# One attention break per step: transposes, next scores and older values behind a unit

## The reference

```python
def diff_attention(q1, q2, k1, k2, v, lam):          # 4 heads, 64 wide; v 128 wide
    ...
        def probs(q, k):
            s = jnp.einsum('bhqd,bhkd->bhqk', q, k).astype(jnp.float32) * scale
            return jax.nn.softmax(jnp.where(mask, s, NEG_INF), axis=-1)

        att = probs(qb1, k1) - lam * probs(qb2, k2)   # one block of 128 queries
        return jnp.einsum('bhqk,bhkd->bhqd', att.astype(v.dtype), v)

# in each of the two layers
    proj = u @ w_in[i]
    ...
    o = diff_attention(q1, q2, k1, k2, v, lam)
    o = rms_norm_2(o, sub_norm_g[i]) * (1.0 - lam_init)
    ...
    merged = (g_a * (y_a @ w_pool_out[i])
              + g_b * (y_b @ w_conv_out[i])
              + g_c * (y_c @ w_attn_out[i]))
    h = h + merged @ w_o[i]
```

## Time and profile before

| | |
|---|---|
| median of 3 runs | 2577.78 us (2577.49 to 2578.59) |
| the profiled execution's own time | 2577.84 us |
| its span in the trace | 2576.1 us |
| PE busy | 2558.5 us, 99% of the span |
| DVE, POOL, ACT busy | 1486.3, 1514.9, 838.6 us |
| `L_MIX` and `L_MERGE` up to the last turn_out | about 966 to 1240 us (layer 0), 1804 to 2075 us (layer 1) |

### The profile page before, as it was taken

One profiled execution on the slowest core, in us unless ns is written; L12 is line 12 of the kernel. 1 busy time (PEld: TensorE's weight loads), 2 busy tenths in 40 slices (PEclk: granted clock), 3 DMA queues, 4 the chain that ended last, 5 costly groups with the idle time before them and its releaser, 6 DMA issues.

```text
span 2576.1 us, 32876 instructions
## 1 busy us (share of the span) xinstructions
PE 2558.5 (99%) x11723; PEld 2062.5 (80%) x11723; DVE 1486.3 (58%) x2084; ACT 838.6 (33%) x1157; POOL 1514.9 (59%) x1820
## 2 busy tenths in 40 slices
PE   8999999999999999999999999999999999999999
PEld 7767778888888887778888888888778888888887
DVE  7756774487474737845583442754773448344275
ACT  5444442233222343354321111134334432111112
POOL 7634446666666755555565655765554556565576
PEclk9999999999999999999999999999999999999999
DMA  5311113222222332222322222233222222222223
GB/s 208 115 66 50 55 61 131 98 83 98 99 97 98 109 111 82 83 82 82 106 99 98 98 97 92 89 114 105 77 85 84 82 106 98 99 98 97 92 89 130
DMA packets 36829, 247.44 MB, mean 96 GB/s; under 512 B 4464, under 2 KB 4848, under 8 KB 7792
## 3 DMA queue, kind: packets, MB, share of 16 engines
q1 hardware_dynamic: 34704, 238.57, 26.2%
q10 hardware_dynamic: 2016, 7.35, 0.8%
HBM read 243.81 MB, written 2.10 MB: 95 GB/s over the span
## 4 chain that ended last, share of the span: by engine, by line
PE 31%; POOL 30%; issue 22%; DVE 0%; POOLq 0%; DMA 0%; ACT 0%; DVEq 0%; SPq 0%; ACTq 0%
POOL w_lo L377 30%; PE bank L832 7%; PE bank L834 7%; PE bank L833 7%; PE both L833 3%; PE both L834 3%; PE both L832 3%; PE bank L1281 0%; PE both L1257 0%; PE bank L1243 0%; PE bank L1241 0%; PE bank L1242 0%; DMA raw<-stream 0%; POOLq L415 0%; POOLq L374 0%
## 5 line engine op out<-in xcount | busy, mean ns | idle before, releaser
L377 POOL TENSOR_TENSOR w_lo<-raw,w_hi 128x256 fp32r<-128x256 f32 x1784 | 1492.6, 868 | 964.2 <-ACT w_hi L434 963.2
L434 ACT ACTIVATE w_hi<-raw 128x1024 fp32r<-128x1024 f32 x446 | 469.1, 1056 | 981.6 <-PE bank L834 476.8
L832 PE MATMUL bank<-a_hi,w_hi 128*128 128x512 f32 x1440 | 582.1, 404 | 0.0
L834 PE MATMUL bank<-a_hi,w_lo 128*128 128x512 f32 x1440 | 562.3, 390 | 0.0
L833 PE MATMUL bank<-a_lo,w_hi 128*128 128x512 f32 x1440 | 561.3, 390 | 0.0
L832 PEld LDWEIGHTS bank<-a_hi,w_hi 128*128 128x128 f32 x1440 | 270.5, 188 | 63.7 <-issue 10.3
L834 PEld LDWEIGHTS bank<-a_hi,w_lo 128*128 128x128 f32 x1440 | 270.3, 188 | 58.3
L833 PEld LDWEIGHTS bank<-a_lo,w_hi 128*128 128x128 f32 x1440 | 270.9, 188 | 54.7 <-issue 3.1
L832 PE MATMUL bank<-y_hi,w_hi 128*128 128x512 f32 x696 | 272.4, 391 | 0.0
L834 PE MATMUL bank<-y_hi,w_lo 128*128 128x512 f32 x696 | 270.9, 389 | 0.0
L833 PE MATMUL bank<-y_lo,w_hi 128*128 128x512 f32 x696 | 270.8, 389 | 0.0
(11 more groups left out here) (343 smaller groups left out, 3279.6 us busy)
## 6 DMA issues: line engine op xcount, KB each, us to landing
raw<-stream SPq DMA_DIRECT2D x223, 1024.0 KB, 4.8
h<-xT SPq DMA_DIRECT2D x8, 256.0 KB, 5.9
h<-xT ACTq DMA_DIRECT2D x1, 2048.0 KB, 8.1
outT<-h SPq DMA_DIRECT2D x8, 256.0 KB, 2.3
h<-decay ACTq DMA_DIRECT2D x1, 1024.0 KB, 4.8
h<-rope ACTq DMA_DIRECT2D x1, 1024.0 KB, 9.3
prob<-pT ACTq DMA_DIRECT2D x2, 512.0 KB, 4.4
par<-par ACTq DMA_DIRECT2D x2, 408.0 KB, 3.3
```

The source lines that it names most:

```text
L377: pool.tensor_tensor(w_lo[:, s, part], raw[:, s, part], w_hi[:, s, part], ALU.subtract).then_inc(lo_done, 1)
L434: act.activation(w_hi[:, s, cols], raw[:, s, cols], ACT.Copy).then_inc(hi_done, 1)
L832: pe.matmul(dst, w_hi[:, s, cols], rhs_hi(k), start=start and k == 0, stop=False)
L834: ins = pe.matmul(dst, w_lo[:, s, cols], rhs_hi(k), start=False, stop=stop and k == nk - 1)
```

## The change

Three things move, in both layers; no instruction is added or removed.

- The transposes of step s leave the inside of the unit. Behind the unit stand now, by the new function `attention_place`, the transposes of s, the scores of s+1 and the values of s-1. Only for step 15 does the place lie inside a unit (n = 23), and values(15) follow behind that unit.
- As the values of a head's last step come one step later, the head's parts move: `attention_out` and `head_root` by two slots (head 0) or three units (heads 1 and 2), `head_norm` from iterations k = 9, n = 2, n = 14 to k = 11, n = 6, n = 18, `turn_out` from slot 10, n = 3, n = 15 to slot 12, n = 7, n = 19, `head_out` with it. Head 3 stays.
- `turn_out` and the late norm's sum, which write `b_cmp`, now also wait until ACT has copied the transposes in front.

```diff
@@ -761,7 +761,7 @@
                     if k == 0:
                         load_table(ACT.Exp)
                         attention_step(0)
-                    if k == 8:
+                    if k == 10:
                         head_root()
                         load_table(ACT.Exp)
                     if k % 2 == 1:
@@ -772,7 +772,7 @@
                     if n < 24 and n % 3 == 0:
                         attention_step(8 + n // 3)
                     ahead(ub, j)
-                    if n in (1, 13, 25):
+                    if n in (4, 16, 25):
                         head_root()
                     if (layer, n) == (0, 9):
                         load_table(ACT.Sqrt)
@@ -1260,7 +1260,7 @@

                 def attention_transposes(s):

-                    if s > 1 and s % QT == 1:
+                    if s > 2 and s % QT == 2:
                         pe.wait_ge(head_out_split, layer * LAYER_HEADS + s // QT)
                     if (layer, s) == (0, 11):
                         pe.wait_ge(late_root_ready, 1)
@@ -1272,8 +1272,6 @@
                 def attention_values(s):

                     hd, i = s // QT, s % QT
-                    if s < 15:
-                        attention_scores(s + 1)
                     pe.wait_ge(probs_copied, ptr.due())
                     if i == 0:
                         pe.wait_ge(attention_out_read, ofree.due())
@@ -1283,8 +1281,17 @@
                                         skip_group_check=True)
                     ins.then_inc(values_added, pv.up())

+                def attention_place(s):
+
+                    attention_transposes(s)
+                    if s < 15:
+                        attention_scores(s + 1)
+                    if s > 0:
+                        attention_values(s - 1)
+
                 def turn_out(hd):

+                    pe.wait_ge(probs_copied, ptr.now() + (hd < 3))
                     pe.wait_ge(head_scaled, layer * LAYER_HEADS + hd + 1)
                     for i in range(QT):
                         ins = pe.transpose(b_cmp[:, i * P:(i + 1) * P], tile_c[:, i * P:(i + 1) * P], ident)
@@ -1298,10 +1305,8 @@
                 def mixed(slot, k):


-                    if k == 1 and slot == 10:
+                    if k == 1 and slot == 12:
                         turn_out(0)
-                    if k == 5 and slot % 2 == 1:
-                        attention_transposes(slot // 2)
                     if k == 3 and slot in (3, 4, 6, 8):
                         pe.wait_ge(to_transpose, tin.due())
                         g = 3 if slot == 3 else 4 - slot // 2
@@ -1313,17 +1318,18 @@
                     unit(ul + L_MIX, slot, 2, [bank[slot % 2][:, :]], a_op(), 8,
                          lambda k, slot=slot: mixed(slot, k))
                     if slot % 2 == 1:
-                        attention_values(slot // 2)
+                        attention_place(slot // 2)

                 def merged_beside(n, k):


-                    if (n, k) in ((3, 2), (15, 2), (26, 5)):
+                    if (n, k) in ((7, 2), (19, 2), (26, 5)):
                         turn_out(1 + n // 12)
                     if (layer, n) == (0, 9) and k == 1:
+                        pe.wait_ge(probs_copied, ptr.now() + 1)
                         square_sum(b_cmp, src=tile_d)
-                    if n < 24 and n % 3 == 2 and k == (3 if n % 6 > 3 else 5):
-                        attention_transposes(8 + n // 3)
+                    if (n, k) == (23, 3):
+                        attention_place(15)

                 for n in range(36):
                     br, j = n // 12, n % 6
@@ -1338,8 +1344,10 @@
                     else:
                         unit(ub, n % 12, 7 - j, [merge_bank[2 * j - 8][:, :], merge_bank[2 * j - 7][:, :]],
                              y_op(br * 4), 4, beside_n)
-                    if n < 24 and n % 3 == 2:
-                        attention_values(8 + n // 3)
+                    if n < 23 and n % 3 == 2:
+                        attention_place(8 + n // 3)
+                    if n == 23:
+                        attention_values(15)
                 singles(ul + L_WO, 8, y_op(), first=next_y, lags=first_lags, ways=2, late=2)
                 uc = ul + L_MLP
                 singles(uc, 8, a_op(), first=next_a, normed=True)
@@ -2192,15 +2200,15 @@
                         mix_in(k - 1)
                     if k % 2 == 0:
                         step_probs(k // 2)
-                    if k == 8:
+                    if k == 10:
                         attention_out()
                     if k > 0:
                         mix(k - 1)
                     if k in (3, 4, 6, 8):
                         pooled_out(3 if k == 3 else 4 - k // 2)
-                    if k == 9:
+                    if k == 11:
                         head_norm(0)
-                    if k == 10:
+                    if k == 12:
                         head_out(0)
                 mix_in(15)
                 mix(15)
@@ -2248,12 +2256,12 @@
                             head_out(3)
                         if stepped:
                             step_probs(8 + n // 3)
-                        if n in (0, 12, 24):
+                        if n in (3, 15, 24):
                             attention_out()
                         hd = 1 + n // 12
-                        if n < 24 and n % 12 == 2:
+                        if n < 24 and n % 12 == 6:
                             head_norm(hd)
-                        if n < 24 and n % 12 == 3:
+                        if n < 24 and n % 12 == 7:
                             head_out(hd)
                         if layer == 0:
                             late_norm(n)
```

## The result

The changed kernel takes 2594.14 us (median of four runs, 2590.37 to 2595.79); the kernel before took 2577.88 beside it (2577.49 to 2578.59). The ratio is 1.0061 with an interval of 1.0043 to 1.0078: slower by 0.6%, and above the range of 2584.4 to 2593.0, though two of the four runs lie inside it. The four runs lie 5.4 us apart, those of before 1.1. TensorE's granted clock, averaged over a run, was 1.000 in the run of 2590.37, 0.998 in that of 2592.65, and 0.997 in those of 2595.62 and 2595.79.

What follows compares the result with a forecast made beforehand. PE, busy for 2558.5 of 2576.1 us, bounds the kernel. Waits of turn_out (+13.0) and saved breaks (-1.2) give +11.8 us on 2577.84, so 2589.6 us, with a range of 2584.4 to 2593.0.

Steps and rivals of the forecast that it cites:

- lost whole: On PE: whatever makes it stop is lost at its length, since no later wait would take it up.
- third rival: PE resumes at a lower rate behind turn_out's waits, losing 1.6 us per stop: 2592.8 or 2596.0 us; chance 0.10.
- the cheaper form of the lower rate: Only the two 3.1 us waits of head 2 make PE resume slowly: 2589.6 + 3.2 = 2592.8 us.
- The waits of `turn_out`: PE waits for head_norm in each layer: 1.2 (head 0), 2.2 (head 1), 3.1 us (head 2); +13.0 in all.
- Head 0: Slot 12: PE waits 1.2 us for the scaled tile, DVE taking 11.6 us behind step_probs of step 5; lower bound 0.
- The longer wait: Head 2, n = 18: three long DVE instructions could each wait 0.76 us for POOL; 4.3 us, total time 2592.
- first rival: At n = 6 the head is scaled in time, only the breaks remain: 2576.6 us; chance 0.06.
- the forecast's own range: 2587.5 to 2592 us: head 0 between 0.4 and 1.4, head_norm's products short or long; chance 0.65.
- The late norm's sum: Layer 0, n = 9: head_out of head 1 precedes its squares on DVE; taken at 0, at worst 0.69 us once.
- The breaks: Steps 0 to 14 of each layer lose one break of a unit by transposes: 30 times 0.04, -1.2 us.
- Transposes to scores: Scores following directly on transposes on PE: taken at nothing, bounded at 3.3 us; as rival 2592.9 us, chance 0.03.
- The other edits at nothing: ACT's later copy, the w_hi behind it and DVE's lateness in slots 12 to 15: no cost to PE.

Runs made afterwards that it cites:

- e4: Changed kernel with unread identity transposes ahead of PE's wait for the scaled head (7, 19, 28 for heads 0, 1, 2): 2590.1 us, ratio 1.0048.
- e8: e2 with the late norm's squares of tile 4 moved to iteration 2 and of tile 5 to iteration 3 on DVE: 2577.62 us (one run).
- e1: Changed kernel with the transposes of heads 0 to 2 and the late norm's sum later inside the same units on PE: 2577.31 us, ratio 0.9998.
- e5: Changed kernel with transposes of heads 0 to 2 between units (behind slot 12, units 7, 19) and the late norm's sum at k=4: 2576.41 us, ratio 0.9995.
- e2: Changed kernel with DVE's head_norm of heads 1 and 2 ahead of the evacuation of units 6 and 18: 2579.42 us, ratio 1.0007.
- e3: Kernel before, with unread DVE products ahead of the scaling (four for head 1, five for head 2): 2595.41 us, ratio 1.0067.
- e6: Changed kernel with DVE's head_norm of heads 1 and 2 between the evacuation of units 6 and 18 and step_probs: 2582.7 us, ratio 1.0018.
- e7: Kernel before, with unread DVE products ahead of scaling heads 1 and 2: 3 and 6 in layer 0, 8 and 12 in layer 1: 2602.52 us (one run).

## Why the prediction was wrong

**The step that failed** is the price of a stop: "lost whole", so at its length, with nothing in the sum for the slow restart behind it, which took 6.0 us in the profiled run. The prediction had that restart only as its third rival, "the stops cost more than their length", at a chance of 0.10, with the range's upper end at "the cheaper form of the lower rate". Its mechanism decided in three of the four runs. Its price was nearly right: the prediction read 1.6 us per stop from the program's start, which gave 2592.8 to 2596.0; the trace has 1.6, 1.6 and 2.7 (transposes included), and the runs end at 2595.8. What was wrong was to give the likeliest case a stop that costs its length, on no better ground than that the trace had no stop of two or three us in mid program. That absence was no evidence for the cheap case, while the one place in the trace where PE came out of standing still spoke for the dear one. (The distances alone show it there; the profile's granted clock reads 1.00 in that stretch.) The section "Why this matters for your kernels" of the Trainium skill's page "TensorE: Matmul & The Clock Gate" warns of idle stretches. The trace agrees behind three of the four longer stops, with 0.43 us between two products behind one of 2.1 us. e4 shows that work in the gap keeps the clock at 1.0.

**The waits of `turn_out`**: the mechanism was right, six times in PE's list and four of over 2 us. Head 1 measured 2.11 for 2.2, head 2 3.15 for 3.1. For head 1 this was partly luck: the product took 0.69 us, not the 0.90 that was taken, and the 0.15 us from the product's end to PE's start (1116.94 to 1117.09), which the sum left out, made up for most of it. Head 0 was too large, 0.73 for 1.2, a term mis-sized by DVE durations beside POOL: from the end of `step_probs` to the scaled tile it took 10.8 us, not 11.6, since the split took 2.4 for 3.14 and the product 0.69 for 0.90. POOL, which before worked from 1037.06 to 1044.45, now stood still from 1038.94 to 1041.23 and was done at 1045.12. Sum 12.0 for 13.0. The longer wait that the prediction worked out, as a bound, from the section "Who interferes with whom" of the Trainium skill's page "SBUF — State Buffer" (4.3 us for head 2) is not in the trace; the rows' price held. Two slips change nothing: the "four instructions" of the first rival are six, and the forecast's own range ends at 2592, where the conditions that it names reach 2577.84 + 2 x 6.7 - 1.2 = 2590.0.

**The late norm's sum**, taken at 0 and bounded at 0.69 us, cost 1.58. `head_out` is two instructions of 0.75, not one, and it pushed four more, of 1.1 to 1.25 us beside POOL, past the end of unit 8, so that an evacuation and the last squares came late behind them. The bound counted the instruction that was moved, and not the queue behind it at its new place. e8 (one run) confirms it.

**The breaks**, -1.2: e1 without its two waits is 1.4 us below before, and e5 1.3, of which three more breaks in each layer (0.24 by the prediction's price) are not the change's. So -1.1 to -1.4, as forecast, as far as medians can tell: the intervals of both ratios still hold 1. **Transposes to scores**, taken at 0: no loss remains for it in e1 or e5; right. **The other edits at nothing** (the copy on ACT, w_hi, late evacuations in slots 12 to 15): none appears in the list of waits.

Without the clock the terms add up to 2577.8 - 1.2 + 12.0 + 1.6 = 2590.2, which is e4 (2590.1) and the one run at a clock of 1.000 (2590.37), 0.6 above the forecast. That this sum came out so near is luck: heads 1.0 us too dear and a late norm's sum 1.6 us too cheap nearly cancel.

## What to carry to other kernels

Where one engine is busy for 99%, an instruction moved on a second engine is costed by all that stands ahead of it in its new queue and by all that is queued behind it; the loss here was repaired by asking 2 to 5 us later on PE (e1, e5), or, for the longer stops, by DVE's order alone (e2). A stop of PE of over some two us in mid program is costed at its length plus a slow restart, which came behind 9 of 11 such stops in the three traces that have them and took 1.3 to 2.7 us. And a kernel whose runs spread where they did not before is one in which to read the granted clock behind each stop before looking for a second cause. A stop that can't be removed can be filled with work that nobody reads, which here saved 4 of 16 us.

## What the runs showed that I had not expected

Whether a stop brings the lower clock is not settled by its length alone. In e3 one stop of 2.45 us left the granted clock at 1.00 and the next of the same length was followed by 0.57; in the changed kernel one of 3.14 us left it at 1.00 where one of 2.11 brought it to 0.57. Stops of 1.7 us and less left it at 1.00 (e6, e7, the late norm's sum), those of 3.9, 5.3 and 8.3 us were all followed by a fall. What decides in between stays open. Nor is the price set by the length: 1.3 us behind a stop of 3.9, 1.6 behind 5.3, 2.7 behind 8.3, and 2.4, with 0.3 more in the transposes, behind one of 3.15.

What the price does go with is the time for which PE works at the lower level. In the changed kernel, behind head 2 of layer 0 and behind head 1 of layer 1:

```profile
1198.10:1202.90 4.80, 4.80 (x13) 3.80 (x12) 0.00 (x0) 0.00 (x0) 1.10 (x2) 0.50 0.38 159
...
1966.40:1967.80 1.40, 1.40 (x9) 1.23 (x10) 0.00 (x0) 0.00 (x0) 1.40 (x3) 1.00 1.01 427
1967.80:1971.10 3.30, 3.30 (x9) 2.61 (x8) 0.00 (x0) 0.00 (x0) 1.10 (x2) 0.50 0.20 82
```

The first goes on from the restart at 1197.39, some 5.5 us for 2.7 lost. The second begins only 1.4 us behind the restart and lasts 3.3 us, for 1.6 lost. In e7 the slow starts end some 2.8, 3.4 and 5.6 us behind the three longer stops, for 1.3, 1.6 and 2.7. At half the rate about half of that time is lost.
